# A fourth spare home for streamed expert weights, in the residual rows' buffer

## What is computed

```python
def block(h, p, ...):
    m, new_buf, new_state = mixer(rmsnorm(h, g_mix), ...)
    h = h + m
    h = h + hier_moe(rmsnorm(h, g_ffn), w_rg, b_rg, w_re, b_re, w_gate, w_up, w_down)
    gate = jax.nn.sigmoid(rmsnorm(h, g_ple) @ w_ple_gate)
    h = h + (p @ w_ple_proj) * gate

def hier_moe(u, ...):          # cw[:, e] is 0 but for the two experts of a token
    for e in range(32):
        h = jax.nn.silu(x @ w_gate[e]) * (x @ w_up[e])
        y = y + cw[:, e:e + 1] * (h @ w_down[e])
```

## Time and profile before

| | |
|---|---|
| time, median of 3 runs | 840.43 us (836.63 to 842.46) |
| the profiled execution's own time | 840.24 us |
| its span, first to last instruction | 838.4 us |
| mean granted TensorE clock | 0.989 |
| busy: PE, DVE, ACT, POOL | 736.6 (88%), 279.1 (33%), 180.9 (22%), 101.8 (12%) us |
| DMA | 257.30 MB, 307 GB/s over the span |
| chain that ended last | PE 49%, DMA 34%, DVE 6%, ACT 2% |

### The profile page before, as it was taken

The page is one execution under the profiler, slowest core; times in us unless marked ns, Lnnn a source line. Parts: engine busy times, 40 slices in busy tenths (PEclk is TensorE's granted clock), DMA queues, the critical chain, the costliest instruction groups (busy, mean ns, idle before and its releaser), DMA issues.

```text
span 838.4 us, 11322 instructions
## 1 busy us (share of the span) xinstructions
PE 736.6 (88%) x4530; PEld 459.6 (55%) x4530; DVE 279.1 (33%) x498; ACT 180.9 (22%) x278; POOL 101.8 (12%) x159
## 2 busy tenths in 40 slices
PE   8999999999999888989999887777777777778996
PEld 7988899989999823333333322222222222226675
DVE  5554578576431632011010100100100100104875
ACT  7242321223331300011111110000000000004576
POOL 0500000000010212211212121121121121110000
PEclk9999999999999989999999999999999999999998
DMA  9541216451763789999999999999999999996301
GB/s 347 227 178 51 75 64 227 176 210 72 295 222 102 281 319 421 418 428 424 425 425 427 424 427 424 426 427 426 426 428 426 428 426 426 426 427 239 151 27 75
DMA packets 36280, 257.30 MB, mean 307 GB/s; under 512 B 7860, under 2 KB 8420, under 8 KB 22792
## 3 DMA queue, kind: packets, MB, share of 16 engines
q1 hardware_dynamic: 27248, 237.17, 68.9%
q0 software_dynamic: 6896, 18.00, 5.7%
q10 hardware_dynamic: 2096, 1.55, 0.6%
HBM read 249.96 MB, written 15.13 MB: 316 GB/s over the span
## 4 chain that ended last, share of the span: by engine, by line
PE 49%; DMA 34%; DVE 6%; ACT 2%; issue 2%; DVEq 0%; SPq 0%; POOLq 0%; ACTq 0%
DMA arena<-in_w_exp 32%; PE ps L1547 19%; PE ps L1739 15%; PE ps L1756 5%; PE ps L1870 3%; PE ps L1590 1%; DVE xh L1410 1%; PE ps L1665 1%; PE ps L1688 1%; PE ps L1655 1%; DMA region_u<-h_rows,index 1%; DVE region_u L1363 1%; DMA y_rows<-region_v,scol 1%; PE ps L1747 1%; PE ps L1626 0%
## 5 line engine op out<-in xcount | busy, mean ns | idle before, releaser
L1739 PE MATMUL ps<-arena,region_u 128*64 128x512 f32 x960 | 219.2, 602 | 46.2 <-DMA arena<-in_w_exp 45.2
L1739 PEld LDWEIGHTS ps<-arena,region_u 128*64 128x64 f32 x960 | 67.0, 138 | 196.1 <-issue 124.7
L1359 DVE SCALAR_TENSOR_TENSOR region_u<-ps,small,region_u 128x256 f32<-128x256 f32 x32 | 15.5, 484 | 376.6 <-ACT region_u L855 376.6
L1547 PE MATMUL ps<-u_hi,w_hi 128*128 128x260 f32 x448 | 129.8, 290 | 4.6 <-issue 2.3
L1547 PE MATMUL ps<-u_lo,w_hi 128*128 128x260 f32 x448 | 127.3, 284 | 0.0
L1547 PE MATMUL ps<-u_hi,w_low 128*128 128x260 f32 x448 | 127.2, 284 | 0.0
L1756 PE MATMUL ps<-arena,region_u 128*64 128x512 f32 x480 | 109.6, 598 | 6.0 <-DMA arena<-in_w_exp 2.5
L1547 PEld LDWEIGHTS ps<-u_hi,w_hi 128*128 128x128 f32 x448 | 85.1, 190 | 6.5 <-issue 3.9
L1547 PEld LDWEIGHTS ps<-u_hi,w_low 128*128 128x128 f32 x448 | 85.2, 190 | 0.0
L1547 PEld LDWEIGHTS ps<-u_lo,w_hi 128*128 128x128 f32 x448 | 85.0, 190 | 0.2
L676 POOL DMA_INDIRECT y_rows<-region_v,scol x32 | 33.4, 1044 | 367.0 <-ACT region_v L859 367.0
(11 more groups left out here) (275 smaller groups left out, 867.9 us busy)
## 6 DMA issues: line engine op xcount, KB each, us to landing
arena<-in_w_exp SPq DMA_DIRECT2D x88, 2048.0 KB, 26.9
arena<-in_w_in SPq DMA_DIRECT2D x35, 512.0 KB, 3.8
region_q<-in_w_exp SPq DMA_DIRECT2D x24, 256.0 KB, 10.2
arena<-in_w_exp SPq DMA_DIRECT2D x8, 512.0 KB, 4.1
arena<-in_w_ple_gate SPq DMA_DIRECT2D x2, 2048.0 KB, 23.6
region_u<-in_xt SPq DMA_DIRECT2D x2, 1040.0 KB, 6.2
arena<-in_state_ret POOLq DMA_DIRECT2D x2, 1024.0 KB, 8.5
xh<-v_few POOLq DMA_DIRECT2D x1, 2048.0 KB, 9.1
```

The costliest lines, as they stand in the source:

```text
L1359: V.scalar_tensor_tensor(hs[b], ps[:, 2 + b, 256:512], rs[b], sg[b], ALU.mult, ALU.mult).then_inc(out_sem, 1)
L1547: last = mm(halves(out)[:, half, :], w[:, k, :], u[:, cols], start=(k == 0 and s == 0), stop=(k == KD - 1 and s == 2))
L1739: last = mm(ps[side * 64:side * 64 + 64, 2 + b, :], xv[:, k // 4, k % 4, :], rows(k % 4 * 2 + side), start=(k == 0), stop=(k == KD - 1))
```

## The change

There is a fourth spare home, the first 4096 columns of `xh`: the residual rows of tiles 0 to 3 are overwritten by weights once their copy in `h_rows` is complete, and are read back from `h_rows` in the tail, tile by tile. Ten units (0 to 9) now have homes before the first expert. The homes are taken in turn, ring then spares, up to unit 23 (`EARLY_HOMES`), so a unit follows ten behind up to unit 25, and six behind from unit 26.

The second spare is cut into pieces of 512 columns throughout (2 KB a partition); it was loaded in pieces of up to 1536. Units 10 to 13 are loaded in quarters, each as soon as PE has used the quarter that lay there (`piece_used`, counted in `gate_up` and `down` of experts 0 and 1). The waits in front of the spares move: unit 7 and three pieces of unit 8 wait for nothing more, the rest of unit 8 for routing (`lg_ready`) and the last turn of rows, and unit 9 for `h_stored`. The wait for the first gather is gone.

```diff
+EARLY_HOMES = [4, 5, 3, 0, 1, 2, "s0", "s1", "s2", "s3"] * 2 + [4, 5, 3, 0]
+EARLY_PAIRS = len(EARLY_HOMES) // 6
+PIECED = (3, 4, 10, 11, 12, 13)
-SPARES = 3
+SPARES = 4
...
+        def in_pieces(ap, c0):
+            return [(ap[:, n * 512:n * 512 + 512], (c0 + n * 512, c0 + n * 512 + 512)) for n in range(ap.shape[1] // 512)]
-                 [(region_v[:, 1024:2560], (0, 1536)), (region_m[:, spare_m + 512:spare_m + 2048], (1536, 3072))]
+                 in_pieces(region_v[:, 1024:2560], 0) + in_pieces(region_m[:, spare_m + 512:spare_m + 2048], 1536)
...
+                 in_pieces(xh[:, :, :].rearrange("p t c -> p (t c)")[:, 0:4096], 0)]
...
+            for n in range(8):
+                load_spare(1, n)
+            for n in range(3):
+                load_spare(2, n)
+            sp.wait_ge(lg_ready, 1)
+            sp.wait_ge(pe_jobs, HEAD.pe(("tp", KD - 1)))
+            for n in range(3, 8):
+                load_spare(2, n)
             sp.wait_ge(h_stored, 16 * 2 * len(STORES))
-            for n in range(4):
-                load_spare(1, n)
-            sp.wait_ge(xg_loaded[0], 16)
             for n in range(8):
-                load_spare(2, n)
+                load_spare(3, n)
...
+            def wait_home(unit):
+                old = unit - (10 if unit < 26 else 6)
+                sp.wait_ge(used[old % 3], old // 3 + 1)
+            for unit in range(10, 6 * EARLY_PAIRS + 6):
+                home = EARLY_HOMES[unit] if unit < len(EARLY_HOMES) else PAIR_SLOTS[unit % 6]
+                if unit in PIECED:
+                    for n in range(PIECES):
+                        if n < PIECES - 1:
+                            sp.wait_ge(piece_used, (unit - 10) * (PIECES - 1) + n + 1)
+                        else:
+                            wait_home(unit)
+                        load_piece(unit, home, n)
+                    continue
+                wait_home(unit)
...
+            def load_rows(t):
+                sp.dma_start(xh[:, t, :].rearrange("p (n c) -> p n c", n=2), h_full[:, t, :, 0:512]).then_inc(
+                    xh_loaded[t], 16)
             for n, slot in enumerate(GATE_SLOTS):
                 sp.wait_ge(gu_done, NE - 1)
                 sp.dma_start(ring[:, slot, :], a["w_ple_gate"][n]).then_inc(slot_filled[slot], 16)
+                if n == 0:
+                    load_rows(0)
...
                 sp.dma_start(y_buf[n % 2][0:m, :], y_tok[r0:r0 + m, :]).then_inc(y_loaded[n % 2], 16)
+                if 0 < n < NT - 1:
+                    load_rows(n)
...
                 if k == 0:
                     dve.wait_ge(y_loaded[n % 2], 16 * (n // 2 + 1))
+                    if n:
+                        dve.wait_ge(xh_loaded[t], 16)
...
                     if half_sem and k == 3:
                         last.then_inc(half_sem, 1)
+                    elif k < pieces and k < KD - 1:
+                        last.then_inc(piece_used, 1)
```

More of the change, by code:

```diff
@@ L411, in build @@
                                             "stored")}
+        xh_loaded = [sem(f"xh_loaded{t}") for t in range(NT - 1)]
         y_loaded = [sem(f"y_loaded{i}") for i in range(2)]
@@ L423, in chunk_wait, with fills @@
             eng.wait_ge(chunk_loaded[n % WIN_SLOTS], 16 * (n // WIN_SLOTS + int(n % WIN_SLOTS > 0)))
+        def fills(unit, slot):
+            return sum(16 * PIECES if n in PIECED else 16 for n in range(unit + 1) if EARLY_HOMES[n] == slot)
         def pair_fill(i, j):
-            slot = (EARLY_SLOTS[i] if isinstance(i, int) and i < 3 else PAIR_SLOTS)[j]
-            if isinstance(i, int) and i < 3:
-                turn = sum(slot in slots for slots in EARLY_SLOTS[:i + 1])
-                return slot, 16 * turn + (16 * (PIECES - 1) if slot in PIECE_SLOTS else 0)
-            return slot, i * 16 + (16 * (PIECES - 1) if slot in PIECE_SLOTS else 0)
+            if isinstance(i, int) and i < EARLY_PAIRS:
+                home = EARLY_HOMES[i * 6 + j]
+                if home in range(RING):
+                    return home, fills(i * 6 + j, home)
+                return home, 16 * len(spare[int(home[1])]) * EARLY_HOMES[:i * 6 + j + 1].count(home)
+            slot = PAIR_SLOTS[j]
+            return slot, i * 16 + (fills(len(EARLY_HOMES) - 1, slot) - (EARLY_PAIRS - 1) * 16)
         w_pp = region_z[:, 0:2 * D]
@@ L476, in load_first, with load_spare @@
                 for j in units:
[L477 removed]
+                    slot = EARLY_HOMES[j]
                     sp.dma_start(ring[:, slot, :], a["w_exp"][j]).then_inc(slot_filled[slot], 16)
[L480 removed]
+            def load_spare(i, piece, unit=None):
                 ap, (c0, c1) = spare[i][piece]
[L482 removed]
+                unit = 6 + i if unit is None else unit
+                sp.dma_start(ap, a["w_exp"][unit, :, c0:c1]).then_inc(spare_loaded[i], 16)
             def load_xt_again(half):
@@ L1729, in in_spare, with gate_up @@
                 return rows
-            def gate_up(b, units, out_sem, half_sem=None):
+            def gate_up(b, units, out_sem, half_sem=None, pieces=0):
                 xv = xgT[b].rearrange("p (k h r) -> p h k r", h=2, r=ROWS)
@@ L1748, in hidden_t, with down @@
                 last.then_inc(out_sem, 1)
-            def down(b, rows, out_sem):
+            def down(b, rows, out_sem, pieces=0):
                 for q in range(4):
@@ L1757, in down @@
                                   start=(q == 0), stop=(q == 3))
+                    if q < pieces:
+                        last.then_inc(piece_used, 1)
                 last.then_inc(out_sem, 1)
@@ L1767, in pair_of_experts @@
                         slot, filled = pair_fill(i, 3 * b + j)
-                        if slot is None:
-                            j = j % 3
-                            units.append((in_spare(j), spare_loaded[j], 16 * i * len(spare[j])))
+                        if slot not in range(RING):
+                            units.append((in_spare(int(slot[1])), spare_loaded[int(slot[1])], filled))
                         else:
                             units.append((in_ring(slot), slot_filled[slot], filled))
-                    gate_up(b, units, gu_done, gu_half)
+                    gate_up(b, units, gu_done, gu_half, (KD, PIECES)[b] if first else 0)
                     parts = parts_of(i, b)
@@ L1789, in pair_of_experts @@
                         pe.wait_ge(out_ready, e - 1)
-                    down(b, rows, down_done)
+                    down(b, rows, down_done, PIECES - 1 if first and b == 0 else 0)
             pe.wait_ge(act_jobs, HEAD.count("A", len(JOBS)))
```

32 lines of the change are left out of this document (10 added, 22 removed).

## The result

The changed kernel takes 845.67 us (median of 6 runs, 844.82 to 845.94), the kernel before in the same session 839.15 (6 runs). The ratio is 1.0074, with a 95% interval of 1.0054 to 1.0095. The forecast was 837.2 (833.0 to 842.5), so its sign was wrong and the range missed. The profiled execution took 845.83 us with a span of 844.0; before, 840.24 and 838.4.

A forecast was written before the change was run, and what follows sets the result against it. Loads were taken as ahead at first, limited by homes PE gives back, then the weight stream as the bound from 447.80 us. Terms -3.8 + 0.8 + 0 = -3.0 took 840.2 to 837.2 us, range 833.0 to 842.5.

The forecast's parts named there:

- The head start and the ring: Expert weight loads: stream gets ahead, but unit 26 still waits for expert 6's `down`; -3.8 us, bounds -2.0 and -4.0.
- The first quarter: First `gate_up`: unit 10's first quarter goes out about 1.2 us after its start, closing the hole at 300 to 305.
- The rival that the lead could be kept: Expert weight loads: unit 26 goes out earlier and the stream keeps its lead of up to 9 us; 832, chance 0.07.
- The first gather: Before the first expert: gather takes 6.7 us beside pieces instead of 5.9; +0.8 us, bounds 0 and +5.0.
- their 1.6 us: Before the first gather: the last store landed 1.6 us ahead of the index; stores were expected to stay within this.
- The upper bound of +5.0: Before the first expert: at most +3.0 us for a slower first gather and +2.0 for slower stores.
- the rival: Kernel start: stores and gathers wait behind weight pieces, so PE starts later; +5.0 us, 841.4, chance 0.13.
- The tail: After the experts: four read-back loads, 1.2 us each, are hidden; term 0, bounds 0 and +4.9 us.
- the upper bound: Tail: all four read-back loads bare on DVE's path to the end, +4.9 us.
- Late PE: Kernel start: gather at 8.9 us and late stores cost +5.0 us, giving 841.4; worst case 850; chance 0.13.
- the read-back on the path: Tail: all four read-back loads are bare, +4.9 us, giving 842.1; chance 0.07.
- Small pieces: Spare-home loads in 2 KB rows: second round costs nothing, or 2 us if the queue is not ahead of the ring.

The follow-up runs named there:

- run 7: Changed kernel with ACT's four small stores issued by SP, in its own queue ahead of unit 7's pieces: 838.3 us, ratio 1.0001.
- run 2: Changed kernel with the pieces of units 7 and 8 held until ACT's four small stores have landed: 842.11 us, ratio 1.0037.
- Run 1: Changed kernel with the four residual-row read-back loads moved from the tail to where SP would wait for unit 26: 844.1 us, ratio 1.0064.
- run 4: Kernel before the change with only the tail's read-back loads and the additions' waits for them added: 841.81 us, ratio 1.0033.
- run 8: Changed kernel with nine homes kept for four rounds, no read-back, small stores on SP, embedding's parts at pairs 6 to 10: 839.37 us, ratio 0.9992.
- run 9: Changed kernel with small stores issued by SP and ten homes for three rounds, six from unit 36; read-back kept in the tail: 837.7 us, ratio 0.9988.
- run 5: Changed kernel with the second spare in its old pieces of up to 1536 columns (6 KB a partition): 845.92 us, ratio 1.0077.

## Why the prediction was wrong

**The head start and the ring: right.** The term was -3.8 with a pause near 385 to 392 and unit 26 landing 8 to 9 us after its issue. The pause came at 390 to 395 and the load took 7.9 us, so the term was 4.0 where it had been put at 3.8. (The first quarter went out 2.0 us after the start of `gate_up`, at 303.28, and not after 1.2, as the clock was still low; nothing hung on it.) The experts gained 4.8, the rest by the shorter first `gate_up`. In run 7, with nearly the start of before, they gained 4.0: unit 26 landed after 8.4 us, 3.5 less than before, and the first `gate_up` took 9.45, 0.3 less. The rival that the lead could be kept was worth 5 us in the text; a third round gave 1.5.

**The first gather: the step that failed.** The text said "I leave them within their 1.6 us" of the stores, and put +0.8 on the gather. It was the other way round: the gather was no slower, and the stores were late by 5 us. POOL's last landed some 1.6 us later than before (at 286.9 against 285.3), still 0.2 ahead of the index, which was made at 286.87 + 0.25. The four small ones of ACT were rounded up in the upper bound and not looked at by themselves, though the gather waits for them too. They are 1040 packets, which next to a weight stream go one for one with 2 KB packets. Runs 2 and 7 take the delay away in two ways. The upper bound of +5.0 comes near the measured 5.2 by luck: 3.0 of it stood for a slower gather, which cost nothing, and 2.0 for the stores, which cost all of it. The Trainium skill (DMA: Bandwidth & Descriptors, on queues and rings) was cited for the rival: an engine drains a whole packet of some 9 to 17 descriptors from a queue before it turns to the next. The trace agrees that queues take turns, 780 records of 64 bytes in the time of 790 of 2 KB; how many a turn holds it does not show, since equal turns of any length give equal counts.

**The tail: also failed.** The term was 0, "so it is hidden". The argument looked at who waits for the second gate load and for the rows, and both are indeed hidden. It did not look at what else moves beside these loads: the last scatter, whose landing took 1.5 us longer (5.8 against 4.4), and behind which the expert rows and DVE stand. Run 1 takes that away, run 4 brings it into the old kernel. A second part of the 4.9 us is the low clock: 2.4 us on the turns and 64 matmuls (1.97 + 5.17 against 1.09 + 3.64), of which some 2.0 lengthen the tail, as PE had waited 0.4 us behind these matmuls before. The third, some 1.4, is the first tile's expert rows, which were issued 0.3 us later behind the scatter and took 5.9 us (4.8 in run 9); its cause I have not separated.

The clock is a term that the prediction did not have at all, and it is not the read-back's alone: runs 1 and 8 have the low clock without a read-back, with tails of 76.3 and 76.2 us, and run 9 has the read-back without the low clock, with 76.4. So of the 4.9 us of the one pair of profiles the read-back's own share is 1.5 at the high clock (run 9 against before); at the low clock it lies between 1.2 and 3.6 (77.5 to 79.8 in the changed kernel and runs 2, 5 and 7, against 76.2 and 76.3). That 4.9 equals the upper bound is chance: the bound priced four bare loads on DVE's path, and DVE waited for none of them.

**The rivals did not exclude each other.** Late PE (841.4) and the read-back on the path (842.1) had 0.13 and 0.07 as if only one could come. They lie in different stretches, so their prices add: with both of the prediction's upper bounds the sum is 840.2 - 3.8 + 5.0 + 4.9 = 846.3. The measured stretches, 840.2 + 5.45 - 4.8 + 4.9 = 845.8, give the profiled execution's time, as they must.

**Small pieces: nearly right.** They were costed at nothing, and in the first round run 5 shows no gain from longer ones; where the stream was full they moved at 404 instead of 422 GB/s (run 9), some 4% less. In the changed kernel's second round the stream moved at 415 GB/s from 310 to 378 us, at 422 before; the lead that this cost was lost at unit 26 in any case.

## What to carry to other kernels

When a wait is taken away to let bulk loads go early, list every small transfer that the next stage waits for and count its packets, not its bytes: put it into the bulk queue ahead of the loads, or hold the loads until it is in. For bytes added to a tail ask not only who waits for them, but what lands beside them. Rivals that lie in different stretches of the program are terms of one sum, and their chances are not shares of one whole.

## What the runs showed of the hardware

- Two hardware queues with work on the same DMA engines advanced one packet for one: 780 of q10 to 790 of q1 in 4 us beside 2 KB packets, and 184 to 195 in 4 us beside packets mostly of 6 KB (run 5). By an estimate from their shares in the first window, 64 us of engine time times 94.7% and 13.4%, a 2 KB packet took some 77 ns and a 64-byte one some 11 ns. From 282 to 292 us, in which the 1040 went by in the changed kernel, the engines gave 85.1% of their time to the weights, 13.2% to POOL's stores and 7.4% to ACT's.
- The last POOL scatter took 4.3 to 4.4 us with the gate loads alone beside it and 5.3 to 5.9 with a read-back more, whether that stood ahead of the second gate load or behind it. Where the second gate load was the last in front of the expert rows, the scatter landed 0.2 to 0.4 us after it (the changed kernel, before, runs 1, 4, 8 and 9).
- TensorE's clock fell to its lower level, 1.2 GHz (0.51 from 779 to 786 us), in the tail after short idle times of PE (0.92 us and 3.44 us in the rows above, the second in part within the low stretch). The length of the idle time alone does not decide: runs 1 and 8 lost the clock after 1.58 us, before kept it after 1.53, and run 9 kept it after 0.89 and 2.08. What decides stays open. Over the whole span the mean granted clock was 0.981 to 0.986 in all six runs of the changed kernel, and 0.988 or more in 26 of the 27 runs of before that stood beside run 7. That fits longer low stretches in every run of the change, but a mean over the span does not tell where they lie.
